# Scores over cached keys as three fp32r products of halves that are split on chip, the rotary part stacked into one

## The chip, the cores and the metric

One core of one Trainium2 chip runs one inference step of a two-layer streaming encoder. The metric is the device time of one execution, in microseconds (us). Names of engines: PE is TensorE (matmuls; PEld are its weight loads), ACT is ScalarE, DVE is VectorE, POOL is GpSimd, SP is SyncE, which issues most DMAs.

## What is computed

The step has many parts (projections, retention, gated linear attention, windowed attention, two convolutional feed-forward blocks). The change touches one: the latent attention of the eight running requests ("sample"), each with 16 new frames, 8 heads and 1024 cached positions.

```python
def mla_sample(q_nope, q_pe, ckv_all, kpe_all, w_ukv):
    w = w_ukv.reshape(MLA_KV_LORA, MLA_HEADS, MLA_NOPE + MLA_V)
    q_abs = jnp.einsum('bthn,chn->bthc', q_nope, w[..., :MLA_NOPE])
    s = (jnp.einsum('bthc,bkc->bhtk', q_abs, ckv_all, preferred_element_type=jnp.float32)
         + jnp.einsum('bthr,bkr->bhtk', q_pe, kpe_all, preferred_element_type=jnp.float32)) * MLA_SCALE
    p = jax.nn.softmax(s, axis=-1).astype(ckv_all.dtype)
    o_lat = jnp.einsum('bhtk,bkc->bthc', p, ckv_all)
    return jnp.einsum('bthc,chv->bthv', o_lat, w[..., MLA_NOPE:])
```

A request's scores are a 128 x 1152 matrix: 8 heads x 16 frames against 1024 cached keys and 128 new rows (a mask leaves the request's own 16 of them). Each key has 256 latent values (two contractions of 128) and 32 rotary values (one contraction of 32). Everything is float32.

## The kernel before

The program is written by hand, engine by engine, with semaphores. It is a sequence of phases with a barrier between them: latents, prompt attention (`phase_mla_prompt`), sample attention (`phase_mla_sample`), retention and so on. Most large products elsewhere go through `mm3` (L126 to L130): an operand is split into a high half (a copy rounded to fp32r, by ScalarE) and a low half (the operand minus the high half, by VectorE or POOL), and the product is high x high + high x low + low x high. The sample attention did not do this: its products are plain f32 matmuls, each of which the trace records as two.

`phase_mla_sample` (L652) handles request b in steps; every engine runs its own `step(b, s, ...)` through `slots`, where s = b % 2 names the half of each double buffer. The first two and the last steps are written out, the four in the middle are two turns of a loop with register arithmetic. In step b TensorE does, in this order: the scores of request b (two groups of 512 keys, each two latent products and one rotary, then the 128 new keys), the values of request b-2, the transposes of the probabilities of request b-1, the transposes of the output of b-2. The scores of request b wait for the exponential of request b-1 (`ex`), because both use the same PSUM banks.

VectorE takes the maximum of b's scores (L793), multiplies it (L795), prepares the queries of request b+1 (L784 to L787), scales the output of b-2 (L802), and copies half of the transposed probabilities (L805). ScalarE takes the exponential (L766), copies the other half (L769) and the transposed output (L774). SP loads the transposed latent cache and the rotary cache of request b+1 when the scores of b-1 are done (L706 to L714); POOL's queue loads the untransposed cache for the values when the values of b-2 are done (L700). The buffers of the transposed cache lie in the unused right halves of `x_or_mix` and in `cacheT_end`; the rotary rows in partitions 64 to 95 of `mla_tab` and `s_kpeT`. Request 0's are loaded during the prompt phase (L458 to L461).

## Time and profile before

| what | value |
|---|---|
| median of 3 runs | 3146.82 us (3143.75 to 3147.49) |
| the profiled execution's own time | 3143.82 us |
| its span, first to last instruction | 3142.0 us |
| PE busy | 2974.2 us (95%) |
| PE weight loads busy | 2609.2 us (83%) |
| DVE, ACT, POOL busy | 1654.5, 1035.4, 842.5 us (53%, 33%, 27%) |
| mean granted TensorE clock | 0.973 |

The sample attention is the stretch from 323 to 446 us of the span, 4% of it. A share of busy time is an average over stages; what a stage is bound by is read from the timeline and the table of stretches of that stage. Ends of matmuls are modelled, so the pace of a stream of products is read from the distance of their starts, not from their durations. The granted clock is TensorE's, as a share of 2.4 GHz.

### The profile page before, as it was taken

How to read it: one execution, taken by the hardware profiler on the slowest of the kernel's cores; microseconds unless marked ns; L12 is line 12 of the kernel's file. 1: busy time of each engine (PE TensorE's matmuls, PEld its weight loads, DVE VectorE, ACT ScalarE, POOL GpSimd, SP SyncE). 2: the span in 40 equal slices, each digit the busy share in tenths (PEclk: the TensorE clock that was granted, in tenths of full speed). 3: DMA queues.
4: the chain of work that ended last, by engine and by line, in shares of the span. 5: the costliest groups of instructions: out<-in, count | busy, mean ns of one | idle time of the engine just before them, and what ended most of it. 6: DMA issues, size and time to landing. Idle time of an engine off the chain costs nothing. (4 is left out here: it accounts for less than half of the span.)

```text
span 3142.0 us, 42381 instructions
## 1 busy us (share of the span) xinstructions
PE 2974.2 (95%) x15759; PEld 2609.2 (83%) x15759; DVE 1654.5 (53%) x2599; ACT 1035.4 (33%) x2017; POOL 842.5 (27%) x704
## 2 busy tenths in 40 slices
PE   8898889998999999999997898998999999999997
PEld 7455458886899999999996798997889999999996
DVE  3566224666455555555545443455545555555556
ACT  4344122333342322322233344334342222322223
POOL 1245011112233232232235000012132223232235
PEclk9999899998999999999998898999999999999999
DMA  3100330103111111111101111113111111111112
GB/s 125 33 13 4 138 130 18 51 21 119 34 59 40 47 41 46 40 42 45 40 28 72 49 35 39 28 42 116 41 53 47 40 40 40 47 40 47 40 34 79
DMA packets 71943, 160.47 MB, mean 51 GB/s; under 512 B 19258, under 2 KB 33739, under 8 KB 70772
## 3 DMA queue, kind: packets, MB, share of 16 engines
q1 hardware_dynamic: 70676, 150.51, 14.9%
q0 software_dynamic: 1152, 8.39, 0.7%
q8 instruction: 76, 1.25, 0.2%
q14 instruction: 39, 0.32, 0.0%
HBM read 144.42 MB, written 15.11 MB: 51 GB/s over the span
## 5 line engine op out<-in xcount | busy, mean ns | idle before, releaser
L128 PE MATMUL psum<-xT_hi,tk_whi 128*128 128x384 f32 x2112 | 711.6, 337 | 8.5 <-ACT tk_u L2210 4.3
L129 PE MATMUL psum<-xT_lo,tk_whi 128*128 128x384 f32 x2112 | 710.3, 336 | 0.0
L130 PE MATMUL psum<-xT_hi,tk_wlo 128*128 128x384 f32 x2112 | 710.1, 336 | 0.0
L2409 DVE TENSOR_TENSOR x_or_mix<-x_or_mix,psum 128x512 f32<-128x512 f32 x684 | 466.1, 688 | 219.7 <-PE psum L130 219.4
L128 PEld LDWEIGHTS psum<-xT_hi,tk_whi 128*128 128x128 f32 x2112 | 397.6, 188 | 12.5 <-ACT tk_u L2213 6.1
L129 PEld LDWEIGHTS psum<-xT_lo,tk_whi 128*128 128x128 f32 x2112 | 397.5, 188 | 1.6
L130 PEld LDWEIGHTS psum<-xT_hi,tk_wlo 128*128 128x128 f32 x2112 | 397.5, 188 | 0.0
L2372 DVE SCALAR_TENSOR_TENSOR tk_c<-tk_u,tk_cw,tk_c 128x1168 f32<-128x1168 f32 x84 | 120.3, 1433 | 428.1 <-ACT tk_c L2221 428.1
L128 PE MATMUL psum<-tk_dhi,tk_gh 128*128 128x512 f32 x756 | 296.3, 392 | 1.7 <-ACT tk_u L2213 1.7
L129 PE MATMUL psum<-tk_dlo,tk_gh 128*128 128x512 f32 x756 | 296.2, 392 | 0.0
L130 PE MATMUL psum<-tk_dhi,tk_gl 128*128 128x512 f32 x756 | 296.0, 392 | 0.0
L1960 POOL TENSOR_TENSOR tk_wlo<-tk_wraw,tk_whi 128x1024 fp32r<-128x1024 f32 x88 | 231.0, 2626 | 185.8 <-ACT tk_whi L2198 185.8
L1985 POOL TENSOR_TENSOR tk_gl<-tk_g,tk_gh 128x1152 fp32r<-128x1152 f32 x42 | 112.5, 2678 | 511.7 <-ACT tk_gh L2227 511.7
L2227 ACT ACTIVATE tk_gh<-tk_g 128x1152 fp32r<-128x1152 f32 x42 | 49.0, 1166 | 517.1 <-DVE tk_g L2404 517.1
L2374 DVE SCALAR_TENSOR_TENSOR tk_c<-tk_u,tk_cw,tk_c 128x1168 f32<-128x1168 f32 x84 | 209.5, 2495 | 10.9 <-DVE tk_c L2372 4.1
L128 PEld LDWEIGHTS psum<-tk_dhi,tk_gh 128*128 128x128 f32 x756 | 143.1, 189 | 31.1 <-issue 2.3
L130 PEld LDWEIGHTS psum<-tk_dhi,tk_gl 128*128 128x128 f32 x756 | 142.7, 189 | 30.1
L129 PEld LDWEIGHTS psum<-tk_dlo,tk_gh 128*128 128x128 f32 x756 | 142.8, 189 | 28.8
L2210 ACT ACTIVATE tk_u<-psum 128x384 f32<-128x384 f32 x176 | 85.4, 488 | 236.1 <-PE psum L130 236.1
L599 POOL TENSOR_SCALAR mla_p<-mla_p,mla_ri 128x128 f32<-128x128 f32 (+7 forms) x64 | 110.2, 1725 | 190.7 <-DVE mla_ri L628 190.7
L128 PE MATMUL psum<-tk_mix_w,xT_hi 128*128 128x512 f32 x288 | 121.1, 421 | 14.6 <-POOL tk_mix_w L845 7.4
L2212 ACT ACTIVATE tk_u<-psum 128x256 f32<-128x256 f32 x88 | 33.9, 385 | 304.0 <-PE psum L130 303.7
(376 smaller groups left out, 5306.1 us busy)
## 6 DMA issues: line engine op xcount, KB each, us to landing
tk_wraw<-in_w_up SPq DMA_DIRECT2D x88, 512.0 KB, 3.6
tk_draw<-in_w_down SPq DMA_DIRECT2D x44, 512.0 KB, 3.6
s_ckv<-in_c_ckv POOLq DMA_DIRECT2D x8, 1024.0 KB, 5.1
retw_raw<-in_w_ret SPq DMA_DIRECT2D x32, 256.0 KB, 3.5
tk_mix_wraw<-in_w_out SPq DMA_DIRECT2D x16, 512.0 KB, 4.4
glaw_raw<-in_w_gla SPq DMA_DIRECT2D x32, 192.0 KB, 2.9
x_or_mix<-in_xT SPq DMA_DIRECT2D x9, 512.0 KB, 9.8
tk_xin<-in_x_in SPq DMA_DIRECT2D x9, 512.0 KB, 3.4
```

The lines of the kernel that those rows point to most:

```text
L128: nc.tensor.matmul(out, a[0], b[0], start=first, stop=False)
L129: nc.tensor.matmul(out, a[0], b[1], start=False, stop=False)
L130: return nc.tensor.matmul(out, a[1], b[0], start=False, stop=last)
L599: nc.gpsimd.tensor_scalar(p, p, ri[:, u % 4:u % 4 + 1], None, ALU.mult).then_inc(scl, 1)
L1960: nc.gpsimd.tensor_tensor(wlo[:, ab].rearrange("p k n -> p (k n)"), wraw[:, ab, :], whi[:, ab].rearrange("p k n -> p (k n)").bitcast(F), A ...
L1985: nc.gpsimd.tensor_tensor(gl[:, par, :], gf[:], gh[:, par, :].bitcast(F), ALU.subtract).then_inc(gs, 1)
L2210: last = nc.scalar.activation(u[:, ab, 2 + q * GRP:2 + (q + 1) * GRP], PS[:, q, 0:GRP], ACT.Copy)
L2212: nc.scalar.activation(u[:, ab, 2 + 2 * GRP:US], PS[:, 2, 0:SEQ - 2 * GRP], ACT.Copy)
L2227: nc.scalar.activation(gh[:, par, :], gf[:], ACT.Copy).then_inc(ghd, 1)
L2372: nc.vector.scalar_tensor_tensor(cv[:, ab, 2:], u[:, ab, 1:UW - 1], cw[:, ab, col4(j, 1)], cv[:, ab, 2:], ALU.mult, ALU.add).then_inc(cch, 1)
L2374: nc.vector.scalar_tensor_tensor(cv[:, ab, 2:], u[:, ab, 0:UW - 2], cw[:, ab, col4(j, 0)], cv[:, ab, 2:], ALU.mult, ALU.add).then_inc(cvd, 1)
L2409: nc.vector.tensor_tensor(x, x, PS[:, down_bank(n), :], ALU.add).then_inc(ad, 1)
```

## The change

- `c.rounded` places fp32r tensors on top of buffers that exist. High halves of the latent cache lie in the part of `latT` that this phase does not read, low halves replace the raw cache in place, the rotary stack lies in the left part of `mla_kT` and in a new buffer `s_kpe3`, the queries' halves in `mla_wq`, the right part of `mla_kT` and `mla_wk`.
- The four latent products of a request become four `mm3` (12 products). ScalarE makes the high halves (`keys_hi`, four pieces of 512), VectorE the low halves (`keys_lo`).
- The rotary cache is loaded three times, into partitions 0 to 31, 32 to 63 and 64 to 95. ScalarE rounds all 96, POOL (`kpe_lo`) replaces the middle third by its low half: high, low, high. The queries are stacked high, high, low. One product of 96 rows for each 512 keys gives the sum of the three.
- Queries are split the same way (`q_hi`, `queries_lo`).
- The 128 new keys stay plain f32.
- In step b, ScalarE and VectorE split the keys of request b+1 ahead of the exponential and the maximum of request b.
- The values' loads move from POOL's queue to SP's.

The rest of the program is the same. The diff:

```diff
--- before.py
+++ after.py
@@ -67,9 +67,16 @@
 
     def __init__(self, nc, A):
         self.nc, self.A = nc, A
+        self.places = {}
 
     def sb(self, name, shape, dt=F):
-        return self.nc.alloc_sbuf_tensor(name, shape, dt)
+        t = self.nc.alloc_sbuf_tensor(name, shape, dt)
+        self.places[name] = self.nc.sbuf_base - 4 * int(np.prod(shape[1:]))
+        return t
+
+    def rounded(self, name, of, shape):
+
+        return self.nc.alloc_sbuf_tensor_at(name, shape, R, offset=self.places[of])
 
     def sem(self, name):
         return self.nc.alloc_semaphore(name=name)
@@ -458,7 +465,8 @@
                     sp.dma_start(c.XM[:, 6:9, 512:], cache[:, 0:3, :]).then_inc(M.kl[0], 16)
                     sp.dma_start(M.cache_end[:], cache[:, 3, :]).then_inc(M.kl[0], 16)
             sp.wait_ge(pd, DVE_BEFORE[-1])
-            sp.dma_start(M.T[64:96, 0:PAST], A["c_kpeT"][0]).then_inc(M.kl[0], 16)
+            for part in range(3):
+                sp.dma_start(M.T[32 * part:32 * part + 32, 0:PAST], A["c_kpeT"][0]).then_inc(M.kl[0], 16)
 
         @block.tensor
         def _(pe):
@@ -657,7 +665,17 @@
     NK = PAST // P + 1
     ckv = c.sb("s_ckv", [P, 2, NK - 1, 256])
     cacheT = [[c.XM[:, 6 + n, 512:] for n in range(3)] + [M.cache_end[:]], [c.XM[:, n, 512:] for n in range(4)]]
-    kpeT = (M.T, c.sb("s_kpeT", [P, PAST]))
+    latR = c.rounded("s_cacheh", "latT", [P, 4, TOK])
+    XMR = c.rounded("s_cachel", "x_or_mix", [P, NT, D])
+    endR = c.rounded("s_cachel_end", "cacheT_end", [P, 512])
+    KTR = c.rounded("s_kpe3_0", "mla_kT", [P, TOK + 512])
+    cacheH = [[latR[:, 2 * b + i // 2, i % 2 * 512:i % 2 * 512 + 512] for i in range(4)] for b in range(2)]
+    cacheL = [[XMR[:, 6 + n, 512:] for n in range(3)] + [endR[:]], [XMR[:, n, 512:] for n in range(4)]]
+    kraw = (M.T, c.sb("s_kpeT", [P, PAST]))
+    k3 = (KTR[0:96, 0:PAST], c.sb("s_kpe3", [P, PAST], R)[0:96])
+    qh = c.rounded("s_qh", "mla_wq", [P, 2, 2, P])
+    ql = KTR[:, TOK:TOK + 512].rearrange("p (s q n) -> p s q n", s=2, q=2)
+    q3 = c.rounded("s_q3", "mla_wk", [P, 2, P])[0:96]
     qb = c.sb("s_qb", [P, 2, 2, P])
     qpb = c.sb("s_qpb", [P, 2, P])
     Pb = c.sb("s_p", [P, 2, NK * P])
@@ -669,6 +687,10 @@
              "o_transposed", "oT_ready", "uv_done", "dve")
     (ol_, vl0, vl1, qd, sc, nms, ex, tr, pt, pv, orr, otr, otd, uv, dch) = (c.sem("ms_" + s) for s in names)
     rcd = c.sem("ms_reciprocal")
+    names = ("cache_hi", "cache_split", "kpe_hi", "kpe_split", "q_hi", "q_split", "own_mask")
+    (chi, csp, khi, ksp, qhi, qsp, om) = (c.sem("ms_" + s) for s in names)
+    PIECES = (0, 2, 1, 3)
+    came = lambda b, s: b * 32 + 32 if s else b * 40 + 80
     kl, vl = M.kl, (vl0, vl1)
     scored = PS[:, 0:3, :].rearrange("p b n -> p (b n)")[:, 0:NK * P]
 
@@ -694,15 +716,21 @@
         def _(pool):
             for started in (otr, otd):
                 pool.sem_inc(started, 1)
-            for b in range(NB):
-                if b >= 2:
-                    pool.wait_ge(pv, b - 1)
-                pool.dma_start(ckv[:, b % 2], A["c_ckv"][b]).then_inc(vl[b % 2], 16)
+            def kpe_lo(b, s):
+                pool.wait_ge(khi, b + 1)
+                nc.gpsimd.tensor_tensor(k3[s][32:64], kraw[s][32:64, 0:PAST], k3[s][32:64].bitcast(F), ALU.subtract).then_inc(ksp, 1)
+
+            def step(b, s, now, last1, last2):
+                if now and (not isinstance(b, int) or b + 1 < NB):
+                    kpe_lo(b + 1, 1 - s)
+
+            kpe_lo(0, 0)
+            slots(pool, step)
 
         @block.sync
         def _(sp):
             sp.dma_start(M.KT[96:97, 0:NB * P], A["mla_own"]).then_inc(ol_, 16)
-            for b in range(1, NB):
+            def keys(b):
                 if b >= 2:
                     sp.wait_ge(sc, b - 1)
                 cache = A["c_ckvT"][b].rearrange("p q (g n) -> p (q g) n", n=512)
@@ -711,23 +739,42 @@
                 else:
                     sp.dma_start(c.XM[:, 6:9, 512:], cache[:, 0:3, :]).then_inc(kl[0], 16)
                     sp.dma_start(M.cache_end[:], cache[:, 3, :]).then_inc(kl[0], 16)
-                sp.dma_start(kpeT[b % 2][64:96, 0:PAST], A["c_kpeT"][b]).then_inc(kl[b % 2], 16)
+                for part in range(3):
+                    sp.dma_start(kraw[b % 2][32 * part:32 * part + 32, 0:PAST], A["c_kpeT"][b]).then_inc(kl[b % 2], 16)
+
+            def values(b):
+                if b >= 2:
+                    sp.wait_ge(pv, b - 1)
+                sp.dma_start(ckv[:, b % 2], A["c_ckv"][b]).then_inc(vl[b % 2], 16)
+
+            keys(1)
+            values(0)
+            values(1)
+            keys(2)
+            keys(3)
+            for b in range(2, NB):
+                if b + 2 < NB:
+                    keys(b + 2)
+                values(b)
 
         @block.tensor
         def _(pe):
             def step(b, s, now, last1, last2):
                 if now:
-                    pe.wait_ge(kl[s], b * 16 + 16 if s else b * 24 + 48)
-                    pe.wait_ge(qd, b + 1)
+                    pe.wait_ge(qsp, b + 1)
                     ge(pe, ex, b)
-                    for g in range(3):
-                        n = P if g == 2 else 512
+                    for g in range(2):
+                        pe.wait_ge(csp, 4 * b + 2 * g + 2)
                         for q in range(2):
-                            rhs = M.latT[:, 2 + q, TP * P:] if g == 2 else cacheT[s][2 * q + g]
-                            nc.tensor.matmul(PS[:, g, 0:n], qb[:, s, q, :], rhs, start=q == 0, stop=False)
-
-                        rhs = M.KT[64:97, TP * P:TOK] if g == 2 else kpeT[s][64:96, g * 512:(g + 1) * 512]
-                        last = nc.tensor.matmul(PS[:, g, 0:n], qpb[64:97 if g == 2 else 96, s, :], rhs, start=False, stop=True)
+                            i = 2 * q + g
+                            mm3(nc, PS[:, g, :], (qh[:, s, q], ql[:, s, q]), (cacheH[s][i], cacheL[s][i]), q == 0, False)
+                        if g == 0:
+                            pe.wait_ge(ksp, b + 1)
+                        nc.tensor.matmul(PS[:, g, :], q3[:, s], k3[s][:, g * 512:(g + 1) * 512], start=False, stop=True)
+                    pe.wait_ge(om, b + 1)
+                    for q in range(2):
+                        nc.tensor.matmul(PS[:, 2, 0:P], qb[:, s, q, :], M.latT[:, 2 + q, TP * P:], start=q == 0, stop=False)
+                    last = nc.tensor.matmul(PS[:, 2, 0:P], qpb[64:97, s, :], M.KT[64:97, TP * P:TOK], start=False, stop=True)
                     last.then_inc(sc, 1)
                 if last2:
                     pe.wait_ge(pt, 2 * b - 2)
@@ -760,7 +807,23 @@
 
         @block.scalar
         def _(act):
+            def keys_hi(b, s):
+                act.wait_ge(kl[s], came(b, s))
+                for i in PIECES:
+                    nc.scalar.activation(cacheH[s][i], cacheT[s][i], ACT.Copy).then_inc(chi, 1)
+                nc.scalar.activation(k3[s], kraw[s][0:96, 0:PAST], ACT.Copy).then_inc(khi, 1)
+
+            def q_hi(b, s):
+                act.wait_ge(qd, b + 1)
+                for part in range(3):
+                    nc.scalar.activation(q3[32 * part:32 * part + 32, s], qpb[64:96, s, :], ACT.Copy)
+                nc.scalar.activation(qh[:, s], qb[:, s], ACT.Copy).then_inc(qhi, 1)
+
             def step(b, s, now, last1, last2):
+                more = now and (not isinstance(b, int) or b + 1 < NB)
+                if more:
+                    q_hi(b + 1, 1 - s)
+                    keys_hi(b + 1, 1 - s)
                 if now:
                     act.wait_ge(nms, b + 1)
                     nc.scalar.activation(Pb[:, s, :], scored, ACT.Exp, bias=nm[:, s:s + 1], scale=MLA_SCALE, accum_out=rs[:, s:s + 1]).then_inc(ex, 1)
@@ -775,26 +838,45 @@
                                                     PS[:, 7, q * P:(q + 1) * P].rearrange("p (h t) -> p h t", h=MLA_H), ACT.Copy)
                     last.then_inc(otd, 1)
 
+            q_hi(0, 0)
+            keys_hi(0, 0)
             slots(act, step)
 
         @block.vector
         def _(dve):
-            def prepare(b, s):
-
-                nc.vector.tensor_copy(M.KT[96:97, TP * P:TOK], M.KT[96:97, bass.ds(b * P, P)])
+            def own_mask(b):
+
+                nc.vector.tensor_copy(M.KT[96:97, TP * P:TOK], M.KT[96:97, bass.ds(b * P, P)]).then_inc(om, 1)
+
+            def queries(b, s):
                 for q in range(2):
                     nc.vector.tensor_copy(qb[:, s, q, :].rearrange("p (h t) -> p h t", h=MLA_H), M.qabs[:, q, :, bass.ds(b * ST, ST)])
                 nc.vector.tensor_copy(qpb[64:96, s, :].rearrange("p (h t) -> p h t", h=MLA_H),
                                       M.qpe[64:96, :, bass.ds(b * ST, ST)]).then_inc(qd, 1)
 
+            def queries_lo(b, s):
+                dve.wait_ge(qhi, b + 1)
+                nc.vector.tensor_tensor(ql[:, s], qb[:, s], qh[:, s].bitcast(F), ALU.subtract)
+                nc.vector.tensor_tensor(q3[64:96, s], qpb[64:96, s, :], q3[64:96, s].bitcast(F), ALU.subtract).then_inc(qsp, 1)
+
+            def keys_lo(b, s):
+                for n, i in enumerate(PIECES):
+                    dve.wait_ge(chi, 4 * b + n + 1)
+                    nc.vector.tensor_tensor(cacheL[s][i], cacheT[s][i], cacheH[s][i].bitcast(F), ALU.subtract).then_inc(csp, 1)
+
             def step(b, s, now, last1, last2):
+                more = now and (not isinstance(b, int) or b + 1 < NB)
+                if more:
+                    queries(b + 1, 1 - s)
+                    queries_lo(b + 1, 1 - s)
+                    keys_lo(b + 1, 1 - s)
                 if now:
                     dve.wait_ge(sc, b + 1)
                     nc.vector.tensor_reduce(out=mx[:, s:s + 1], in_=scored, axis=AX.X, op=ALU.max).then_inc(dch, 1)
                     dve.wait_ge(dch, b + 1)
                     nc.vector.tensor_scalar(nm[:, s:s + 1], mx[:, s:s + 1], -MLA_SCALE, None, ALU.mult).then_inc(nms, 1)
-                    if not isinstance(b, int) or b + 1 < NB:
-                        prepare(b + 1, 1 - s)
+                    if more:
+                        own_mask(b + 1)
                 if last2:
                     dve.wait_ge(pv, b - 1)
                     dve.wait_ge(rcd, b - 1)
@@ -807,7 +889,10 @@
 
             nc.vector.memset(qpb[96:97], 1.0)
             dve.wait_ge(ol_, 16)
-            prepare(0, 0)
+            own_mask(0)
+            queries(0, 0)
+            queries_lo(0, 0)
+            keys_lo(0, 0)
             slots(dve, step)
             dve.wait_ge(uv, 1)
             nc.vector.tensor_copy(c.XM[:, TP, 0:512], PS[:, 0, :])
```

The loop of the middle steps on VectorE, before: one step, from the maximum (L793) over the preparation of the next queries to the scaling of the output. REGISTER_ALU and ISA rows are address arithmetic.

```order
L793 TENSOR_REDUCE s_mx<-psum 128x1
L795 TENSOR_SCALAR s_nm<-s_mx 128x1
L784 ISA
L784 COPY mla_kT<-mla_kT 1x128
L786 ISA
L786 COPY s_qb<-q_abs 128x128
L786 ISA
L786 COPY s_qb<-q_abs 128x128
L787 ISA
L787 COPY s_qpb<-q_pe 32x128
L799 REGISTER_ALU
L802 TENSOR_SCALAR s_olat<-psum,s_ri 128x256
```

The same loop in the changed kernel: `s_kpe_0_3445` in the first row is the low half of the queries, `s_q_3447` the rotary queries' stack, `s_cachel` the low pieces.

```order
L859 TENSOR_TENSOR s_kpe_0_3445<-s_qb,s_qh 128x256
L860 TENSOR_TENSOR s_q_3447<-s_qpb,s_q_3447 32x128
L864 ISA
L865 TENSOR_TENSOR s_cachel<-x_or_mix,s_cacheh 128x512
L864 REGISTER_ALU
L865 TENSOR_TENSOR s_cachel<-x_or_mix,s_cacheh 128x512
L864 REGISTER_ALU
L865 TENSOR_TENSOR s_cachel<-x_or_mix,s_cacheh 128x512
L864 REGISTER_ALU
L865 TENSOR_TENSOR s_cachel<-x_or_mix,s_cacheh 128x512
L875 TENSOR_REDUCE s_mx<-psum 128x1
L877 TENSOR_SCALAR s_nm<-s_mx 128x1
```

The query copies and six subtractions now stand ahead of the maximum (L875), each low piece behind a wait for its high piece.

ScalarE's loop, before: the exponential (L766), the copy of transposed probabilities (L769), the output's copies (L774).

```order
L766 ACTIVATE s_p,s_rs<-psum,s_nm 128x1152
L768 REGISTER_ALU
L769 ACTIVATE s_pT<-psum 128x640
L774 ISA
L774 ACTIVATE q_abs<-psum 128x8x16
L774 ISA
L774 ACTIVATE q_abs<-psum 128x8x16
```

ScalarE's loop in the changed kernel, one step from its start:

```order
L819 ACTIVATE s_q_3447<-s_qpb 32x128 x3
L820 ACTIVATE s_qh<-s_qb 128x256
L811 ISA
L813 ACTIVATE s_cacheh<-x_or_mix 128x512 x4
L814 ACTIVATE s_kpe<-s_kpeT 96x1024
L829 ACTIVATE s_p,s_rs<-psum,s_nm 128x1152
L831 REGISTER_ALU
L832 ACTIVATE s_pT<-psum 128x640
```

Three copies of rotary queries, one of queries, four pieces and the rotary stack (L814) stand ahead of the exponential (L829) of the request before.

## Rows read from the trace of the kernel before

**Rows 1.** The page's head: the span and the busy time of TensorE.
```profile
span 3142.0 us, 42381 instructions
...
PE 2974.2 (95%) x15759; PEld 2609.2 (83%) x15759; DVE 1654.5 (53%) x2599; ACT 1035.4 (33%) x2017; POOL 842.5 (27%) x704
```

**Rows 2.** The table of stretches: from:to, length, busy us per engine (instructions), clock, DMA.
```profile
323.00:337.19 14.19, 11.65 (x18) 4.03 (x18) 1.08 (x5) 0.00 (x0) 1.31 (x2) 0.64 0.63 231
337.19:351.42 14.23, 11.19 (x19) 4.06 (x20) 2.32 (x6) 1.31 (x2) 0.00 (x0) 0.64 0.24 83
351.42:364.82 13.40, 11.46 (x28) 4.42 (x28) 3.17 (x8) 1.91 (x3) 0.00 (x0) 0.75 0.26 90
...
401.38:413.46 12.08, 12.08 (x48) 7.33 (x48) 3.56 (x9) 2.35 (x5) 0.53 (x1) 1.00 0.54 185
...
425.54:446.00 20.46, 17.15 (x110) 14.35 (x110) 5.17 (x10) 3.84 (x10) 0.53 (x1) 1.00 0.14 51
```

**Rows 3.** The timeline of TensorE over one request: start us, us, engine, line.
```profile
401.28 3.72 PE L737 MATMUL psum<-s_ckv,s_pT 128*128 128x256 f32 x16
...
406.47 1.88 PE L727 MATMUL psum<-x_or_mix,s_qb 128*128 128x512 f32 x4
...
412.30 0.71 PE L727 MATMUL psum<-latT,s_qb 128*128 128x128 f32 x4
...
413.36 0.92 PE L737 MATMUL psum<-s_ckv,s_pT 128*128 128x256 f32 x3
```

**Rows 4.** The same view where fp32r products of 512 columns run (clock 1.00, then 0.50).
```profile
59.60 0.39 PE L128 MATMUL psum<-wlat_hi,xT_hi 128*128 128x512 f32 x1
59.82 0.39 PE L129 MATMUL psum<-wlat_lo,xT_hi 128*128 128x512 f32 x1
...
453.49 0.63 PE L129 MATMUL psum<-retw_lo,xT_hi 128*128 128x512 f32 x1
453.91 0.63 PE L130 MATMUL psum<-retw_hi,xT_lo 128*128 128x512 f32 x1
```

**Rows 5.** Copies and subtractions of such widths: timeline, groups, and two source lines (min/median/max ns).
```profile
450.79 2.19 ACT L110 ACTIVATE retw_hi<-retw_raw 128x512 fp32r<-128x512 f32 x4 [7.85 <-POOL ret_qTm L959]
...
L2198 ACT ACTIVATE tk_whi<-tk_wraw 128x1024 fp32r<-128x1024 f32 x88 | 91.6, 1043 | 0.0
...
L2213 ACT ACTIVATE tk_u<-psum 128x128 f32<-128x128 f32 x88 | 24.1, 274 | 0.0
...
L1123 DVE TENSOR_TENSOR retw_lo<-retw_raw,retw_hi x16: 677/884/1761, 452.0 to 658.2; 128x512 fp32r<-128x512 f32 x16
...
L1960 POOL TENSOR_TENSOR tk_wlo<-tk_wraw,tk_whi x88: 2395/2700/3102, 857.5 to 3060.4; 128x1024 fp32r<-128x1024 f32 x88
```

**Rows 6.** The timeline of the other engines over the same request as rows 3.
```profile
401.39 1.36 DVE L793 TENSOR_REDUCE s_mx<-psum 128x1 f32<-128x1152 f32 x1 [6.25 <-PE psum L730]
401.97 0.61 SPq L714 DMA_DIRECT2D s_kpeT<-in_c_kpeT  x1
...
402.97 1.22 ACT L766 ACTIVATE s_p<-psum,s_nm 128x1152 f32<-128x1152 f32 x1 [7.55 <-DVE s_nm L795]
403.20 0.36 DVE L786 COPY s_qb<-q_abs 128x128 f32 x2
...
406.45 0.69 DVE L805 COPY s_pT<-psum 128x512 f32<-128x512 f32 x1 [0.50 <-PE psum L742]
```

**Rows 7.** The source line of the rotary caches' DMAs: issue to landing.
```profile
L714 SPq DMA_DIRECT2D s_kpeT<-in_c_kpeT x4: 608/615/617, 324.0 to 402.0; - x4
...
DMA to landing us min/median/max: 4.7/5.5/6.6
```

**Rows 8.** The timeline of TensorE where the scores of requests 0, 1 and 2 begin.
```profile
325.51 3.75 PE L727 MATMUL psum<-x_or_mix,s_qb 128*128 128x512 f32 x4 [3.51 <-DVE s_qpb L787]
...
340.23 3.75 PE L727 MATMUL psum<-x_or_mix,s_qb 128*128 128x512 f32 x4 [3.07 <-ACT s_p L766]
...
354.47 2.67 PE L727 MATMUL psum<-x_or_mix,s_qb 128*128 128x512 f32 x4 [1.94 <-ACT s_p L766]
```

## The prediction

> **What bounds the kernel now.** I read the head of the page first. TensorE is busy 95% of a span of 3142.0 us [rows 1], so a gain has to come out of TensorE's own time or out of a wait in the stage that changes. Then the table of stretches over that stage, the sampled requests' attention (323 to 446 us), cut at the ends of the score groups of each request [rows 2]. I write S(b) for the end of request b's scores: S(0) 337.19, S(1) 351.42, S(2) 364.82, then one every 12.1 us up to S(7) 425.54. In a steady stretch TensorE is busy 12.08 of 12.08 us at full clock (2.4 GHz), with VectorE at 3.56 us, ScalarE at 2.35 us and POOL at 0.53 us. There the stage is bound by TensorE alone. In the first three stretches the granted clock is 0.64, 0.64 and 0.75 (partly 1.2 GHz), and TensorE waits some 2 to 3 us in each.
>
> Next the timeline of one request on TensorE [rows 3]. The values, the transposes and the transposes of the output take 401.28 to 406.47, 5.19 us. The six f32 products over the cache (four latent, two rotary; each shows as two records) take 406.47 to 412.30, 5.83 us. The request's own 128 keys end at 413.36, 1.06 us. Sum 12.08.
>
> **What the change removes and adds on TensorE.** The six f32 products become twelve fp32r products of 512 columns (high by high, high by low, low by high) and two of 96 rows for the rotary part. fp32r products of that shape start 0.22 to 0.23 us apart at full clock and 0.42 us apart at half clock [rows 4]; I take 0.229 and 0.427. 14 x 0.229 = 3.21 us in place of 5.83, so 2.62 us less, and a request costs 12.08 - 2.62 = 9.46 us; I take 9.5, for three waits inside the stream that had been none. The own keys stay f32 and unchanged, as do values and transposes. The Trainium skill (FP8 and Floating Point Precision, TensorE Precision Notes) has true f32 at four passes: by that 24 passes against 14, an estimate of 2.3 us saved in place of 2.6, and a result 2 us later. The trace disagrees by the 0.3 us that each request's six products take beyond 24 times the fp32r pace, and the measured row decides.
>
> **What it adds elsewhere, per request.** ScalarE: three copies of 32x128, one of 128x256, four of 128x512, one of 96x1024. The rows give 0.27 us for a 128-wide copy (some 0.22 apart when queued), 2.19 us for four 128x512 in a row, 1.04 us for 1024 wide [rows 5]; the 256-wide one lies between the first two, 0.4. Sum 0.7 + 0.4 + 2.2 + 1.0 = 4.3, and ScalarE goes from 2.35 to 6.7 of 9.5 us. VectorE: one subtraction of 128x256 (0.4), one of 32x128 (0.3), four of 128x512. A subtraction of that width is 0.68 us at least, 0.88 in the median, 1.76 at most [rows 5]; I take 0.69, because POOL is idle when they run. Sum 3.5, VectorE from 3.6 to 7.1. POOL: one 32x1024 subtraction, 2.4 to 3.1 us by the 128x1024 row [rows 5]. SP: two more rotary DMAs of 128 KB per request, and the values' DMAs, which were on POOL's queue. None of these sums reaches 9.5 us, so by load TensorE remains the bound. But they hang one behind the other, and behind them, in ScalarE's and VectorE's queues, stand the exponential and the maximum of the request before. That is what the order pieces show, and what decides.
>
> **The chain between two requests**, in us after S(b-1), for the keys of request b+1 (the buffer comes free at S(b-1)). Waiting cover first: VectorE copies the transposed probabilities from 5.17 for 0.69 and inverts, done at 6.0 [rows 6]; the query copies (0.36 and 0.2) end at 6.6; ScalarE's high halves of the queries end at 7.7. The DMA: today the single rotary DMA is issued at 0.7 and lands 5.5 us later [rows 6, 7], at 6.2; two more issues and 256 KB more add 0.8 to 1.8 us, landing at 7.0 to 8.0. Both ends meet at about 7.7. High pieces until 9.9, rotary high until 11.0. Low pieces on VectorE follow from 8.4 at 0.69 each, until 11.1. S(b) comes at 9.5, so the maximum of request b starts 1.6 us late, at 11.1; the exponential starts 1.58 after it and takes 1.22 [rows 6], done at 13.9. TensorE can start the scores of b+1 only then; but it is busy with values and transposes until 9.5 + 5.2 = 14.7. So the lateness is covered by 0.8 us. In terms of a period: 13.9 plus 4.3 of scores is 18.2 us for two requests, 9.1 for one, against TensorE's 9.5. POOL's rotary low half is done at 11.0 + 2.6 = 13.6 and needed at 16; covered.
>
> **The start.** Today TensorE begins at 325.51 [rows 8]. Now the queries' high halves (1.1), low halves (0.7) and two low pieces (1.4) come first: 328.8. The 14 products at half clock take 14 x 0.427 = 6.0; POOL's first low half is ready only at 332.6, a wait of 1.3; the own keys at half clock about 1.9. S(0) = 338.0, 0.8 us later than now. The exponential is done and the next scores start 3.0 us after that (as today: 337.19 to 340.23 [rows 8]), at half clock 6.0 + 1.9 us: S(1) = 349. Scores of request 2 start 3.1 us later (today 351.42 to 354.47 [rows 8]) and take between 4.3 (full clock) and 7.9 (half); I take 5.9, since that stretch is mixed today: S(2) = 358.0. Today it is 364.82, so 6.8 us are gained by then.
>
> **The sum.** Requests 3 to 7: today 425.54 - 364.82 = 60.7 us, then 5 x 9.5 = 47.5, 13.2 us less. With 6.8 that is 20.0 us; less 0.5 for the added register instructions between VectorE's pieces, 19.5. What follows S(7) (20.5 us of values and output) is unchanged, and the next stage starts at a barrier, so the gain goes through whole. The profiled execution took 3143.82 us and would take 3124.3; the median of the runs, 3.0 us above it, gives 3146.82 - 19.5 = **3127.3 us**.
>
> **Rivals.** (1) **The chain binds.** VectorE's last low piece starts at about 10.4 and POOL's rotary subtraction at 11.0; a VectorE that is 0.6 us later finds POOL at work. In the trace such pieces took up to 1.76 us [rows 5], 1.1 more than alone, in a stage in which POOL subtracts the other half of the pieces. A whole 2.6 us in the way makes 18.2 + 2.6 = 20.8 for two requests, 10.4 for one: 5 x 0.9 = 4.5 us less gain, 3131.8; with a late landing too, 11.0 and 3135. For it: the small margin. Against it: VectorE has only finished pieces in front of it. The Trainium skill (SBUF — State Buffer, Who interferes with whom) states this as a rule: a VectorE instruction with two SBUF inputs and a GpSimd instruction that reads SBUF exclude each other for a whole instruction. By that rule the wait is all of POOL's instruction or none.
> (2) **Slower: the clock falls.** If the chain grows until TensorE idles about 2 us in each request, as it does for 1.94 us in the stretch before S(2) [rows 8], whose granted clock was 0.75, requests run at 1.2 GHz: scores 7.9 and the rest 5.19 x 1.85 = 9.6, together 17.5 us. Five of them are 87.5, 27 us more than today, less the 6.8: 3167. It decides from a period of 11.4 on, a chain of 22.8 us for two, 4.6 over my figure; all four pieces at 1.76 (4.3 more) come near. Against it: POOL has one instruction per request, not one per piece.
> (3) **The products are no faster.** Were they paced like the two records of an f32 product at full clock, 14 x 0.427 = 6.0 in place of 5.83, the stage would lose some 2 us: 3149. Against it: the kernel's other stages run on thousands of such products at the fast pace.
> (4) **The clock comes earlier.** TensorE at 2.4 GHz from request 1 on takes 3.6 us off S(1) and 1.6 off S(2): 3122.
>
> **How the numbers follow.** Forecast 0.50, (1) 0.34, (2) 0.04, (3) 0.03, (4) 0.09. A measurement of this kernel can tell about 0.2%, 6.3 us, from no change. The forecast, (1) and (4) are all beyond it on the fast side: 0.92 with a little off for a noisy median; same 0.04, slower 0.04. The range goes from just under (4), 3121, to just over (1) with a late landing, 3136.
>
> **What would show it.** Right: a period of 9.4 to 9.7 us between score groups, 14 products at 0.229, TensorE busy throughout it, S(7) near 406. The maximum on VectorE starting 1 to 2 us after the scores' end, after the last low piece. Wrong: TensorE idle before the first cache product of each request, released by the exponential (rival 1, with a low piece of over 2 us in front); a granted clock below 1.00 after S(3) (rival 2); products 0.4 us apart (rival 3).

## The result and the profile after

The changed kernel takes 3125.22 us, median of 5 runs (3120.51 to 3130.74). The kernel before, run beside it, takes 3145.53 (5 runs). The ratio is 0.9936, 95% interval 0.9921 to 0.9952: 20 us less, where 19.5 were forecast. Two further sets of the same kernel, run beside the experiments, gave 0.9931 [0.9908, 0.9954] and 0.9925 [0.9913, 0.9938].

The head of the page of after:

```profile
span 3120.7 us, 42590 instructions
...
PE 2948.2 (94%) x15775; PEld 2616.9 (84%) x15775; DVE 1684.6 (54%) x2647; ACT 1071.0 (34%) x2089; POOL 854.9 (27%) x704
```

Against [rows 1] the span is 21.3 us shorter and TensorE 26 us less busy. The stage's first DMA and the next stage's first one, by the timeline of SP:

```profile
322.50 0.23 SPq L732 DMA_DIRECT2D mla_kT<-in_mla_own  x1
...
424.65 1.75 SPq L112 DMA_DIRECT2D retw_raw<-in_w_ret  x4
```

So the stage is 102.15 us long. Before, the same two issues stood at 323.11 and 446.87, 123.76 us. What stands ahead of the stage is 0.6 us shorter and what follows it 0.9 longer (2696.0 us against 2695.1), so the difference lies in the stage, -21.6 us. That the rest came out so nearly equal in these two executions is chance: in the three profiled executions of the changed kernel the span outside the stage differs by up to 10 us with the same code. Below I therefore compare stage lengths as well as totals; the changed kernel's own three profiled stages are 102.15, 102.68 and 101.67.

The table of stretches of after, cut at its own S(b), the end of request b's scores (columns as in [rows 2]):

```profile
323.00:337.03 14.03, 8.25 (x20) 5.88 (x20) 9.88 (x19) 8.72 (x18) 2.84 (x2) 0.54 0.74 254
337.03:346.43 9.40, 6.37 (x22) 5.00 (x21) 5.09 (x12) 5.20 (x11) 1.94 (x1) 0.60 0.51 153
346.43:355.90 9.47, 7.07 (x31) 5.56 (x30) 6.57 (x15) 6.00 (x13) 2.33 (x1) 0.82 0.49 154
355.90:365.30 9.40, 9.40 (x51) 8.03 (x50) 6.69 (x15) 6.30 (x15) 2.34 (x1) 1.00 0.83 266
...
384.40:393.80 9.40, 9.40 (x51) 8.02 (x50) 7.15 (x16) 6.72 (x15) 2.38 (x1) 1.00 0.81 263
...
403.30:424.00 20.70, 17.13 (x110) 14.33 (x110) 5.15 (x10) 3.84 (x10) 0.00 (x0) 1.00 0.16 51
```

From S(2) on one request takes 9.40 us, TensorE busy in all of it at full clock: it is still the bound, with VectorE now at 6.7 to 7.2 and ScalarE at 6.3 to 6.7. (One of the five periods, S(3) to S(4), where TensorE's loop starts its second turn, is 9.72; before, the one there was 12.41; VectorE and ScalarE are at 7.5 and 7.0 in it. In one of the three profiled executions S(2) to S(3) took 10.9, see the experiments.) The stretch behind S(7) is what it was.

TensorE between S(4) and S(5), a request of 9.40 us, by its timeline, which answers to [rows 3]:

```profile
374.95 3.72 PE L784 MATMUL psum<-s_ckv,s_pT 128*128 128x256 f32 x16
...
379.92 0.38 PE L795 MATMUL psum<-ident,s_olat 128*128 128x128 f32 x2
380.06 0.48 PE L135 MATMUL psum<-s_cacheh,s_qh 128*128 128x512 f32 x1
380.37 0.40 PE L136 MATMUL psum<-s_cachel,s_qh 128*128 128x512 f32 x1
...
383.17 0.40 PE L773 MATMUL psum<-s_kpe,s_q 96*128 96x512 f32 x1
383.40 0.61 PE L776 MATMUL psum<-latT,s_qb 128*128 128x128 f32 x4
...
384.35 3.72 PE L784 MATMUL psum<-s_ckv,s_pT 128*128 128x256 f32 x16
```

The fourteen products take 380.06 to 383.40, 3.34 us (0.23 us each, the first one 0.31), in place of 5.83. No idle time is recorded between them. The values and transposes ahead of them take 5.11 us (5.19 before), the own keys behind them 0.95 (1.06 before). VectorE over the request before it:

```profile
364.46 1.89 DVE L865 TENSOR_TENSOR s_cachel<-x_or_mix,s_cacheh 128x512 fp32r<-128x512 f32 x3
366.27 0.68 DVE L865 TENSOR_TENSOR s_cachel_end<-cacheT_end,s_cacheh 128x512 fp32r<-128x512 f32 x1
366.88 1.35 DVE L875 TENSOR_REDUCE s_mx<-psum 128x1 f32<-128x1152 f32 x1
...
368.44 0.81 DVE L849 COPY mla_kT<-mla_kT 1x128 f32 x1
369.43 0.48 DVE L884 TENSOR_SCALAR s_olat<-psum,s_ri 128x256 f32<-128x256 f32 x1 [0.18 <-PE psum L784]
370.41 0.69 DVE L887 COPY s_pT<-psum 128x512 f32<-128x512 f32 x1 [0.50 <-PE psum L789]
...
373.11 0.43 DVE L859 TENSOR_TENSOR s_kpe<-s_qb,s_qh 128x256 fp32r<-128x256 f32 x1 [1.44 <-ACT s_qh L820]
373.55 0.28 DVE L860 TENSOR_TENSOR s_q<-s_qpb,s_q 32x128 fp32r<-32x128 f32 x1
373.87 2.50 DVE L865 TENSOR_TENSOR s_cachel<-x_or_mix,s_cacheh 128x512 fp32r<-128x512 f32 x4
```

The maximum of request 3 starts at 366.88, 1.58 us after S(3) = 365.30, right behind the last low piece, as forecast (1.6). What I had not read off is how little room is left in this column: VectorE waits for TensorE 0.18 us before the scaling of the output (L884) and 0.50 before the copy of the transposed probabilities (L887). Its only other long wait, 1.44, is for ScalarE's query halves, and these hang on VectorE's own query copies. So a turn of VectorE, from one maximum to the next, has 0.68 us to spare (0.97 in the turn that starts at 376.28, beside TensorE's longer request), and TensorE stands directly behind it, since the output's transposes (L795) and then the next scores wait for the scaling.

### The profile page after: what moved, and what is told of

Its sections match the earlier page's. It is cut to its first block and busy times, and to the rows that moved or that the text cites. A ratio compares the mean times of both kernels' runs of the same rounds, so it can differ in the third digit from the quotient of the medians.

```text
span 3120.7 us, 42590 instructions
## 1 busy us (share of the span) xinstructions
PE 2948.2 (94%) x15775; PEld 2616.9 (84%) x15775; DVE 1684.6 (54%) x2647; ACT 1071.0 (34%) x2089; POOL 854.9 (27%) x704
## 5 line engine op out<-in xcount | busy, mean ns | idle before, releaser
L135 PE MATMUL psum<-tk_mix_w,xT_hi 128*128 128x512 f32 x288 | 120.9, 420 | 14.5 <-POOL tk_mix_w L930 7.4
```

Of the source, the lines that this page charges most:

```text
L135: nc.tensor.matmul(out, a[0], b[0], start=first, stop=False)
```

## The experiments

The totals of eleven runs and their ratios against the kernel before run beside them (3145.97, 3146.72 and 3147.91 us in the three sets), with the stage cut into its parts by each trace, in us. Start: first DMA of the stage to S(0).

```
                 median (runs)  ratio [95%]               start S(0)-S(2) S(2)-S(7) stage
before           3145.53 (5)                              14.04   27.65     60.69   123.76
changed          3125.22 (5)    0.9936 [0.9921, 0.9952]   14.53   18.89     47.32   102.15
changed_again    3125.89 (4)    0.9931 [0.9908, 0.9954]   14.78   18.93     47.55   102.68
changed_third    3122.89 (5)    0.9925 [0.9913, 0.9938]   12.13   19.30     48.82   101.67
rotary_f32       3137.11 (10)   0.9972 [0.9958, 0.9985]   12.65   20.13     57.34   111.53
latent_f32       3129.79 (4)    0.9941 [0.9920, 0.9961]   11.16   17.84     50.55   100.98
values_on_pool   3126.16 (4)    0.9930 [0.9913, 0.9947]   14.50   20.22     47.34   103.50
stack_first      3137.19 (10)   0.9974 [0.9964, 0.9984]   14.29   20.08     56.93   112.72
chain_plus_2     3140.44 (10)   0.9980 [0.9968, 0.9993]   16.29   21.70     55.68   115.10
chain_plus_5     3159.88 (4)    1.0048 [1.0031, 1.0065]   19.57   24.84     69.03   134.86
earlier_start    3124.41 (4)    0.9930 [0.9913, 0.9946]   12.52   18.82     47.98   100.73
first_plain      3122.19 (5)    0.9927 [0.9914, 0.9940]    8.90   21.54     47.90    99.76
two_plain        3120.17 (6)    0.9925 [0.9910, 0.9940]    8.91   22.40     47.77   100.50
```

**The changed kernel again**, beside each set of the other runs.

> The changed kernel once more, as the reference for the three runs beside it. Every theory expects its own result again: about 3125 us, and in the trace a period of 9.4 us between the score groups of requests 3 to 7 at full clock.

> The changed kernel once more, for the totals of the two beside it: 3125, stage 102 to 103 long, one request 9.4.

Both came out as expected, apart from the third's stage, 0.3 under its band, and one of its periods. In the third one S(0) came 2.4 us sooner after the stage's start, but VectorE was at request 1's pieces until 342.0, 2.1 us after S(0), so that the exponential came later: S(0) to S(1) took 11.9, S(1) to S(2) 7.4. S(2) to S(3) then took 10.9, with TensorE waiting 1.18 us for the scaling of the output (L795 behind L884): in this execution the changed kernel itself stood behind VectorE for once. The parts of the start shift by up to some 3 us from run to run, the whole stage by 1.

**Which part of the change brings the gain: the rotary stack taken out.** The rotary rows are not stacked; their product is f32 over 32 rows, as before, and POOL has nothing to subtract.

```
...
-                        nc.tensor.matmul(PS[:, g, :], q3[:, s], k3[s][:, g * 512:(g + 1) * 512], start=False, stop=True)
+                        nc.tensor.matmul(PS[:, g, :], qpb[64:96, s, :], kraw[s][64:96, g * 512:(g + 1) * 512], start=False, stop=True)
...
```

> Undoes the rotary part alone (one load of the rotary rows, plain f32 product of 32 rows, no stack on ScalarE, POOL or in the queries); latent products stay split. If TensorE's own stream bounds the stage: two fp32r products of 0.229 us become two f32 products of 0.96 to 1.05, so the period goes from 9.40 to 10.9 to 11.0 us and the whole is 12 to 13 us slower than the changed kernel (about 3138). If instead the chain through DMA, ScalarE and VectorE were what bounds it, a shorter chain (no stack, two DMAs fewer) would leave the period or shorten it.

Measured: period 11.4, 0.4 above the expectation, and 3137.11 in all, as expected. One of the two f32 products of 32 rows in TensorE's timeline of this run (two records), and what follows it:

```profile
387.67 1.12 PE L767 MATMUL psum<-s_kpeT,s_qpb 32*128 32x512 f32 x2
388.72 0.50 PE L135 MATMUL psum<-s_cacheh,s_qh 128*128 128x512 f32 x1
389.06 0.39 PE L136 MATMUL psum<-s_cachel,s_qh 128*128 128x512 f32 x1
```

1.05 us from its start to the next, where the stacked product takes 0.23, and the fp32r product behind it takes 0.34 in place of 0.23: 2 x 0.93 = 1.9 by these rows, 2.0 by the period. TensorE has no idle time in it. The stack, two of the fourteen products, brings 2.0 of the 2.67 us per request (12.07 - 9.40).

**The latent split taken out.** The rotary stack stays; the latent products are plain f32 over the raw cache, and ScalarE and VectorE have no pieces.

```
...
-                        pe.wait_ge(csp, 4 * b + 2 * g + 2)
                         for q in range(2):
-                            i = 2 * q + g
-                            mm3(nc, PS[:, g, :], (qh[:, s, q], ql[:, s, q]), (cacheH[s][i], cacheL[s][i]), q == 0, False)
+                            nc.tensor.matmul(PS[:, g, :], qb[:, s, q, :], cacheT[s][2 * q + g], start=q == 0, stop=False)
...
```

> Undoes the latent part alone (plain f32 products over the raw cache, no cache pieces on ScalarE and VectorE); the rotary stack stays. If TensorE's stream bounds the stage: twelve products of 0.229 become four of 0.91 to 0.96, so the period goes from 9.40 to 10.3 to 10.5 us and the whole is 6 to 9 us slower than the changed kernel, less up to 2 us for an earlier start (about 3131). If the chain bounds it: a period of 9.4 or less, and no slower. The sum of the two undone parts should be the 2.6 us a request that the change saves: more than half of it from the rotary stack, though that is the smaller product.

Measured: period 10.05, better than expected, and a stage of 100.98 us, **shorter than with the split**. Twelve fp32r products in place of four f32 ones save 0.65 us per request (the twelve take 12 x 0.23 = 2.8), and the two savings add up: 2.0 + 0.65 = 2.65 of the 2.67. But request 0 has nothing to hide the splitting behind: S(0) comes 11.16 after the stage's start and not 14.5, and S(0) to S(2) is 1.05 shorter, in spite of the slower products. The clock is full in a stretch in which the changed kernel has 0.83. The row of this run in the table of stretches (19.7 to 29.7 us after its stage's start), and then that of after (24.5 to 34.5):

```profile
347.00:357.00 10.00, 8.06 (x37) 5.24 (x36) 4.02 (x10) 3.54 (x7) 1.94 (x1) 1.00 0.50 147
```
```profile
347.00:357.00 10.00, 7.60 (x31) 5.99 (x30) 7.10 (x16) 6.41 (x13) 2.38 (x2) 0.83 0.47 146
```

So against this run the split gains 3.2 us behind S(2) and loses 4.4 ahead of it (1.7 and 2.4 by the third trace of the changed kernel). The totals of four runs each cannot tell the two kernels apart (0.9941 and 0.9931, intervals 0.004 wide); the stage, 0.7 to 1.7 us, is one trace against three.

**The queue of the values.** The values' DMAs back on POOL's queue, the keys' on SP's alone.

```
...
-                sp.dma_start(ckv[:, b % 2], A["c_ckv"][b]).then_inc(vl[b % 2], 16)
+                pool.dma_start(ckv[:, b % 2], A["c_ckv"][b]).then_inc(vl[b % 2], 16)
...
```

> The loads of the values' cache go back to POOL's queue, behind the rotary subtraction; all else as changed. My theory: the queue that issues them does not matter, since they land some 10 us before they are used: period 9.4, total within noise of the changed kernel. Rival: part of the gain comes from taking them off POOL's queue; then VectorE's pieces or the loads would be late, period above 9.6, and 2 us or more slower.

Measured: period 9.41, S(2) 1.3 us later, total the same. The move of the DMAs between queues has no part in the steady gain.

**POOL's subtraction against VectorE's.** The stacked rows are rounded ahead of the four pieces, so that POOL subtracts while VectorE does.

```
+                nc.scalar.activation(k3[s], kraw[s][0:96, 0:PAST], ACT.Copy).then_inc(khi, 1)
                 for i in PIECES:
                     nc.scalar.activation(cacheH[s][i], cacheT[s][i], ACT.Copy).then_inc(chi, 1)
-                nc.scalar.activation(k3[s], kraw[s][0:96, 0:PAST], ACT.Copy).then_inc(khi, 1)
```

> ScalarE rounds the rotary stack before the four cache pieces in place of after them, so POOL's rotary subtraction runs while VectorE subtracts its pieces. If the two engines exclude each other for a whole instruction: VectorE's first piece waits out POOL's 2.35 us, the chain grows by 1.0 (the stack ahead) plus 1.75, less the slack of 0.7, over two requests: period 9.4 + 1.0 = 10.4, some 5 to 6 us slower in all. If they do not exclude each other: only the 1.0 counts, period 9.55, 1 us slower, which no total can show; the trace would show low pieces of 0.69 us beside POOL's instruction.

POOL and VectorE in this run:

```profile
380.06 2.35 POOL L721 TENSOR_TENSOR s_kpe<-s_kpeT,s_kpe 32x1024 fp32r<-32x1024 f32 x1 [8.90 <-ACT s_kpe L812]
```
```profile
380.53 4.24 DVE L865 TENSOR_TENSOR s_cachel<-x_or_mix,s_cacheh 128x512 fp32r<-128x512 f32 x4 [0.75 <-ACT s_cacheh L814]
384.69 1.34 DVE L875 TENSOR_REDUCE s_mx<-psum 128x1 f32<-128x1152 f32 x1
...
386.26 0.22 DVE L849 COPY mla_kT<-mla_kT 1x128 f32 x1
386.51 0.48 DVE L884 TENSOR_SCALAR s_olat<-psum,s_ri 128x256 f32<-128x256 f32 x1
```

Four pieces take 4.24 in place of 2.50, the first alone 2.43: it starts 0.47 us behind POOL's subtraction and stands until that ends at 382.41. The rule cited in rival (1) (the Trainium skill, SBUF — State Buffer, Who interferes with whom: the two exclude each other for a whole instruction) agrees with these rows: the wait is what is left of POOL's 2.35 us, here 1.88. In the period it costs more than I expected: 14.45, 9.78, 11.12, 10.73 and 10.85 us, 11.4 in the mean, in place of 10.4. VectorE's turns from maximum to maximum are steadier: 10.85 to 11.25 in all but the first two. TensorE's waits in this run show behind whom it stands:

```profile
PE psum L135 <- ACT s_p L829: 8.2, 4, 5.7
PE psum L795 <- DVE s_olat L884: 6.0, 5, 3.0
```

Of the 8.2 us behind the exponential (`ex`), 7.7 are the waits of requests 1 and 2 (5.71 and 2.02). The steady requests wait for the scaled output, not for the exponential, as my chain had it. By VectorE's turn: its first piece waits for ScalarE 0.75 us, the pieces take 1.74 more, the mask copy 0.6 less; of these 1.9, 0.68 are spare, and 9.4 + 1.2 = 10.6. The wait for the query halves, 1.78 us in the next turn in place of 1.44, makes it 10.9.

**The chain lengthened.** Before each of ScalarE's four pieces one further 128x512 copy into an unused place (in the second kernel two), each waited for, so that nothing but the chain grows.

```
...
+                    for k in range(1):
+                        nc.scalar.activation(scratch, M.wuv[:, 0, :], ACT.Copy).then_inc(pad, 1)
+                        act.wait_ge(pad, b * 4 + n * 1 + k + 1)
                     nc.scalar.activation(cacheH[s][i], cacheT[s][i], ACT.Copy).then_inc(chi, 1)
...
```

> One copy of 128x512 (into an unused place, of no use) ahead of each of ScalarE's four high pieces, each waited for: the chain grows by 4 x 0.65 = 2.6 us, TensorE's own stream is untouched. My theory (two requests per turn of the chain, 0.7 us of slack): period 9.40 + (2.6 - 0.7)/2 = 10.35, 5 to 6 us slower than the changed kernel, with about 1 us of TensorE idle before each request's scores, released by the exponential. Rival (one request per turn): period 9.4 + 1.9 = 11.3. Rival (the slack is more than I read): no change.

> Two such copies ahead of each piece: the chain grows by 5.2 us. My theory: period 9.40 + (5.2 - 0.7)/2 = 11.65, about 12 to 13 us slower, TensorE idle for some 2.2 us per request. If TensorE's clock falls to half at such gaps (the rival of the prediction on the slow side): a granted clock below 1.00 in the stretches of requests 3 to 7, scores of 7 to 8 us in place of 4.2, and a period above 12.

This decides between the two pictures of the chain. VectorE in the first kernel:

```profile
375.19 1.35 DVE L880 TENSOR_REDUCE s_mx<-psum 128x1 f32<-128x1152 f32 x1
...
376.76 1.24 DVE L854 COPY mla_kT<-mla_kT 1x128 f32 x1
378.03 0.48 DVE L889 TENSOR_SCALAR s_olat<-psum,s_ri 128x256 f32<-128x256 f32 x1
378.44 0.68 DVE L892 COPY s_pT<-psum 128x512 f32<-128x512 f32 x1
...
382.29 0.69 DVE L870 TENSOR_TENSOR s_cachel<-x_or_mix,s_cacheh 128x512 fp32r<-128x512 f32 x1 [0.46 <-ACT s_cacheh L818]
...
385.85 0.69 DVE L870 TENSOR_TENSOR s_cachel<-x_or_mix,s_cacheh 128x512 fp32r<-128x512 f32 x1 [0.49 <-ACT s_cacheh L818]
386.45 1.35 DVE L880 TENSOR_REDUCE s_mx<-psum 128x1 f32<-128x1152 f32 x1
```

The two waits for TensorE are gone, and the turn from maximum to maximum is 11.26 us; the others between the second and the seventh maximum are 11.00, 11.27, 11.88 and 11.28. TensorE's periods are uneven (10.1, 13.2, 9.4, 11.8, 11.2) with a mean of 11.1. The first piece waits 0.46, the four take 4.25 in place of 2.50, the mask copy 1.24 in place of 0.81: 2.6 us more in a turn, and 9.4 + 2.6 - 0.7 = 11.3. Had a chain of two requests bound, 18.2 + 2.6 would have given 10.4. The second kernel's turns are 13.9 (the first of them 13.6), twice the lengthening: 9.4 + 5.2 - 0.7 = 13.9. So one request costs one turn of VectorE, its waits for ScalarE's pieces included, and the second kernel is slower than the kernel before. One of its stretches and TensorE's waits:

```profile
389.60:403.50 13.90, 11.00 (x47) 8.77 (x46) 7.76 (x16) 11.75 (x23) 2.33 (x1) 0.88 0.54 173
```
```profile
PE psum L797 <- DVE s_olat L889: 12.9, 6, 2.6
```

TensorE waits 2.2 to 2.6 us per request for the output scaling alone, and its mean granted clock is 0.88 in each turn, 1.00 in the changed kernel: part of each request's products stand 0.43 us apart (1.2 GHz), the rest 0.23 (2.4 GHz). The first kernel shows this in one turn, the one above, behind a wait of 1.54 us:

```profile
375.19:386.45 11.26, 9.46 (x41) 7.42 (x41) 7.77 (x16) 9.23 (x19) 2.34 (x1) 0.85 0.57 183
```

**The start made shorter.** In the prologue the queries are copied ahead of the wait for the mask, and ScalarE and VectorE do two key pieces first.

```
...
+            queries(0, 0)
+            keys_lo(0, 0, (0, 1))
+            queries_lo(0, 0)
             dve.wait_ge(ol_, 16)
             own_mask(0)
-            queries(0, 0)
-            queries_lo(0, 0)
-            keys_lo(0, 0)
+            keys_lo(0, 0, (2, 3))
...
```

> Only the first request's order is changed: VectorE prepares the queries before it waits for the mask, ScalarE rounds two cache pieces before the queries and VectorE subtracts them meanwhile. TensorE's first product could start at about 3.3 us after the phase's first instruction in place of 5.7. Theory: 1.5 to 2.5 us less in the stage (S(0) earlier, the rest unchanged). Rival: POOL's rotary low half, not the cache pieces, then sets the end of the first scores, and S(0) moves by less than 1 us. The total can hardly show either; the trace does.

Measured: S(0) after 12.52, stage 100.73, 0.9 to 2.0 us shorter than the changed kernel's three; total 3124.41, not to be told from it. S(0) lies within what the changed kernel shows by itself (12.13 to 14.78), so one trace does not show that the edit brought the difference.

**The version that the runs point to.** The latent products of the first request (or the first two) plain f32, the queries copied ahead of the wait for the mask, the rest as changed.

```
...
+                            if plain(b):
+                                nc.tensor.matmul(PS[:, g, :], qb[:, s, q, :], cacheT[s][i], start=q == 0, stop=False)
+                            else:
                                 mm3(nc, PS[:, g, :], (qh[:, s, q], ql[:, s, q]), (cacheH[s][i], cacheL[s][i]), q == 0, False)
...
```

> Request 0's latent products are plain float32 (no split of its keys or query), requests 1 to 7 and all rotary stacks as in the changed kernel; the queries of request 0 are copied ahead of the wait for the mask. If the split costs its gain only at the stage's start: the scores of request 0 end 10.4 after the stage's start (12.5 to 14.5 in the kernels that split them, 11.2 where all were plain), each later request takes 9.4, so 10.4 + 7 x 9.4 + 21.4 behind the last scores = 97.6 for the stage against 102.2 and 102.7; total 4 to 5 less than the changed kernel run beside it, some 3121. Rival, the start isn't the cost but is made up for by what comes later (TensorE's clock rises when it works, whichever kernel): requests 0 to 2 come closer together but the stage stays at 101 to 102 and the total at 3125.

> As the one beside it, with the latent products of request 1 plain as well. The steady plain request took 10.05 and a split one 9.4, but at the start two plain ones took 8.9 each: S(2) at 28.5 to 29.0 after the stage's start, then 5 x 9.4 + 21.4, together 97 to 97.4, at most 0.6 from the kernel that has one plain request. Rival: the clock has risen by request 1, and the plain one costs 0.65 more than a split one: 98.2.

S(0) came earlier than expected, after 8.90 us, yet the stage is 99.76 and not 97.6: S(0) to S(2) takes 21.54 and not 18.8. With two plain requests it is 100.50, with S(0) to S(2) at 22.40. ScalarE and VectorE of the first kernel show what is late next:

```profile
330.27 2.19 ACT L820 ACTIVATE s_cacheh<-x_or_mix 128x512 fp32r<-128x512 f32 x4 [3.28 <-DMA s_kpeT<-in_c_kpeT]
```
```profile
330.93 2.49 DVE L875 TENSOR_TENSOR s_cachel<-x_or_mix,s_cacheh 128x512 fp32r<-128x512 f32 x4 [2.46 <-ACT s_cacheh L820]
333.35 1.35 DVE L885 TENSOR_REDUCE s_mx<-psum 128x1 f32<-128x1152 f32 x1
```

Request 1's keys land only at 330.2. Its pieces wait for them, and the maximum of request 0, ready at 331.31, stands in VectorE's queue behind the pieces until 333.35. TensorE waits 5.01 us for the exponential. Neither kernel's expectation held, nor its rival's: with one plain request the stage is 1.9 to 2.9 us shorter than the changed kernel's three, where 4 to 5 were hoped for. In the totals nothing can be told: 0.9927 [0.9914, 0.9940] and 0.9925 [0.9910, 0.9940] beside 0.9925 [0.9913, 0.9938] for the changed kernel in the same set. I can't claim a version faster than the changed one.

## Why the prediction was right, and where its steps were not

- **The total: right.** 19.5 us less were forecast, 20.3 measured. Of the 2.1 us between 3127.3 and 3125.22, 1.3 is the kernel before, whose median fell from 3146.82 to 3145.53 with two more runs.
- **TensorE's saving per request: right, with a little luck.** 2.62 was worked out from the pace of other stages' products; 12.07 - 9.40 = 2.67 was measured. The fourteen products save 2.49 of it (3.34 us in place of the forecast 3.21), and the 0.19 that the neighbours gave back had been put at nothing. The 0.5 us for register instructions is not there: S(2) to S(7) lost 13.4 us, 0.7 more than forecast.
- **24 passes against 14 (the Trainium skill, FP8 and Floating Point Precision, TensorE Precision Notes): too little, as the rows said.** It gave 2.3 us. The runs add where the rest sits. An f32 product of 32 rows takes 1.05 us from its start to the next, more than four fp32r products at 0.23 (0.92), and its neighbours lose some 0.1 us each, so the rotary part gains 2.0; a latent f32 product in a row of its like takes 0.86 (two records, each 0.43 us from the next), and three fp32r products take 0.69, so the latent part gains only 0.65. I had treated all six products as alike. In the kernel before, the rotary product between the latent ones:

```profile
408.28 1.12 PE L730 MATMUL psum<-mla_tab,s_qpb 32*128 32x512 f32 x2
409.33 1.12 PE L727 MATMUL psum<-x_or_mix,s_qb 128*128 128x512 f32 x2
```

- **The loads of ScalarE, VectorE and POOL: right.** Forecast 6.7, 7.1 and some 2.6; 6.3 to 6.7, 6.7 to 7.2 and 2.4 were measured. The maximum came 1.6 us after S(b), as said.
- **"18.2 us for two requests, 9.1 for one, against TensorE's 9.5": this step was wrong.** The runs show one turn of VectorE per request. The chain that I followed ended at the exponential. The one that comes last ends at the scaling of the output, which VectorE does after the maximum and the mask copy, and for which TensorE's transposes wait ahead of the next scores. I had counted VectorE's time behind the maximum as nobody's concern. Both pictures leave about the same room, 0.8 and 0.68 us, so the forecast stood. That was luck: nothing in my chain set the 0.68. The price behind the edge is double. An x in each request costs x - 0.7, not half of it, and rival (1) was priced too low: the run that brings it about (stack_first) has periods of 11.4 in the mean and not 10.4, and a total of 3137.19 where the rival said 3131.8. Its reading of the rule, all of POOL's instruction or none, is wrong too: the piece waited out what was left, 1.88 of 2.35 us. The rotary subtraction on POOL stayed out of the pieces' way (366.78 against the last piece's 366.27), by 0.5 us.
- **The start: S(0) 337.03 (338.0 forecast), S(1) 346.44 (349), S(2) 355.91 (358.0).** The first product at 328.35 (328.8) was right. POOL's wait of 1.3 was 0.43. The largest error is S(1), whose products I put wholly at half clock: their spacing falls from 0.43 to 0.23 in the middle of them:

```profile
344.04 0.60 PE L137 MATMUL psum<-s_cacheh,s_kpe 128*128 128x512 f32 x1
344.46 0.41 PE L135 MATMUL psum<-s_cacheh,s_qh 128*128 128x512 f32 x1
344.72 0.40 PE L136 MATMUL psum<-s_cachel,s_qh 128*128 128x512 f32 x1
```

  This is part of rival (4), and it did not last: from 351.6 to 354.6, in request 2, they stand 0.43 apart again, so that the 5.9 us put on those scores was right. Counted from the stage's start, S(2) came 8.3 us sooner than before, 6.8 were forecast: 1.5 of the 2.1 us between 19.5 and the stage's 21.6.
- **Transfers: right in the steady part, unforeseen at the start.** From request 4 on ScalarE never waits for keys. At those of requests 2 and 3 it does, 2.52 and 1.40 us. The first of these costs a little: the maximum of request 1 starts at 346.96, behind the late pieces and 0.5 us after S(1). And late keys are what caps an earlier start, as the kernel with one plain request shows.
- **Rivals (2) and (3)** did not occur: the clock is 1.00 from S(2) on, and the products stand 0.23 us apart. In the lengthened chain, with TensorE idle 2.2 to 2.6 us per request, the clock did fall, but for a part of each request (mean 0.88), and a request took 13.9 us where (2) had 17.5: its price was too high, its direction right.

## What to carry to other kernels

Before you call a chain covered, follow the queue of the helping engine through a whole turn, past the instruction you expect to matter, to the last one that anybody waits for; its waits for the bounding engine, added up, are the room that is left. Ask for each part of a change that speeds up products apart what it saves and what it costs where there is nothing to hide it behind: here two of fourteen products brought three quarters of the gain, and the split of the others paid in 0.65 us steps for a start that cost 2.4 to 4.7.

## What the hardware showed that I had not expected

While POOL subtracts in SBUF, not only VectorE's subtractions stand still but its small SBUF copies as well. The mask copy, one row of 128 values, takes 0.22 us alone (in stack_first, where POOL has long ended, above) and 0.81 here, and two query copies take 2.53 us in place of 0.36 (after):

```profile
366.78 2.38 POOL L721 TENSOR_TENSOR s_kpe<-mla_tab,s_kpe 32x1024 fp32r<-32x1024 f32 x1 [7.48 <-ACT s_kpe L814]
```
```profile
329.23 2.40 POOL L721 TENSOR_TENSOR s_kpe<-mla_tab,s_kpe 32x1024 fp32r<-32x1024 f32 x1 [11.74 <-ACT s_kpe L814]
```
```profile
329.32 2.53 DVE L853 COPY s_qb<-q_abs 128x128 f32<-128x128 f32 x2
```

In both cases VectorE ends just after POOL (369.25 against 369.16; 331.85 against 331.63, with a second copy in the group). In the lengthened chain the mask copy starts 0.5 us sooner within POOL's time and takes 1.24. The maximum, 1.35 us and read from PSUM, runs through POOL's time unchanged (366.88). So 0.6 us of VectorE's turn in the changed kernel is a copy of one row that waits for POOL, nearly as much as the room that the turn has left.
